# Two transformer blocks on one core: the norm's scale read from PSUM, weight splits issued earlier ahead of the norms, and a shared program end

## The reference, cut to what matters

```python
def rmsnorm(x, g):
    xf = x.astype(jnp.float32)
    y = xf * lax.rsqrt(jnp.mean(xf * xf, axis=-1, keepdims=True) + EPS)
    return (y * g.astype(jnp.float32)).astype(x.dtype)
...
    mix = jnp.einsum('bld,de->ble', merged, w_out)
    x = x + rmsnorm(mix, g_post_mix)
    h = rmsnorm(x, g_pre_mlp)
    ff = jnp.einsum('blf,fd->bld', jnp.square(jax.nn.relu(jnp.einsum('bld,df->blf', h, w_ff1))), w_ff2)
    return x + rmsnorm(ff, g_post_mlp)
```

## Time and profile before

| what | us |
|---|---|
| median of three runs | 3706.79 |
| the profiled execution | 3706.02 |
| its span (first to last instruction) | 3704.3 |
| TensorE matmul busy | 3508.4 (95%) |
| VectorE busy | 1446.7 (39%) |
| ScalarE busy | 873.6 (24%) |
| GpSimd busy | 895.3 (24%) |

### The profile page before, as it was taken

How to read it: one execution, slowest core, us unless ns; L and a number is a source line. 1 busy time by engine, 2 the same in 40 slices (tenths; PEclk the granted TensorE clock), 3 DMA queues, 4 the chain that set the end, 5 groups by cost and what they waited for, 6 DMA issues and landing times. The chain is left out here.

```text
span 3704.3 us, 40483 instructions
## 1 busy us (share of the span) xinstructions
PE 3508.4 (95%) x16092; PEld 2820.4 (76%) x16092; DVE 1446.7 (39%) x1591; ACT 873.6 (24%) x1068; POOL 895.3 (24%) x421
## 2 busy tenths in 40 slices
PE   6989999998998999999989998999999899999996
PEld 5767788887876888888867877777777588888885
DVE  7723565655315222212153446463552521121123
ACT  3112222223313111111232222212342411111111
POOL 2101111111341222222312114231245222222223
PEclk9979999999999999999999999999999999999998
DMA  2534343324421111111224213113253211111122
GB/s 109 148 70 158 109 147 126 100 88 167 146 91 73 47 45 51 45 51 45 91 97 124 92 66 120 63 69 125 99 199 136 74 45 51 45 51 45 45 79 102
DMA packets 105056, 336.81 MB, mean 91 GB/s; under 512 B 15232, under 2 KB 25344, under 8 KB 104848
## 3 DMA queue, kind: packets, MB, share of 16 engines
q1 hardware_dynamic: 101344, 329.78, 26.4%
q10 hardware_dynamic: 3584, 5.25, 0.5%
HBM read 250.37 MB, written 87.62 MB: 91 GB/s over the span
## 5 line engine op out<-in xcount | busy, mean ns | idle before, releaser
L270 POOL TENSOR_TENSOR w_lo<-w_raw,w_hi 128x1024 fp32r<-128x1024 f32 x276 | 686.6, 2488 | 2492.2 <-ACT w_hi L268 2492.2
L307 PE MATMUL pair<-act_hi,w_hi 128*128 128x512 f32 x2992 | 971.4, 406 | 18.9 <-issue 7.0
L307 PE MATMUL pair<-act_lo,w_hi 128*128 128x512 f32 x2992 | 946.5, 397 | 0.0
L307 PE MATMUL pair<-act_hi,w_lo 128*128 128x512 f32 x2992 | 945.1, 397 | 0.0
L307 PEld LDWEIGHTS pair<-act_lo,w_hi 128*128 128x128 f32 x2992 | 566.4, 189 | 138.6
L307 PEld LDWEIGHTS pair<-act_hi,w_lo 128*128 128x128 f32 x2992 | 565.4, 189 | 138.7
L307 PEld LDWEIGHTS pair<-act_hi,w_hi 128*128 128x128 f32 x2992 | 547.7, 190 | 142.7 <-issue 23.5
L268 ACT CAST w_hi<-w_raw 128x1024 fp32r<-128x1024 f32 x276 | 288.9, 1047 | 785.9 <-PE pair L307 709.6
L571 DVE TENSOR_TENSOR p<-pair,rs 128x1024 f32<-128x1024 f32 x100 | 122.1, 1221 | 435.6 <-PE pair L307 428.5
L1791 DVE TENSOR_TENSOR f2v<-pair,rs 128x1024 f32<-128x1024 f32 x42 | 51.4, 1224 | 346.6 <-PE pair L307 346.6
L307 PE MATMUL pair<-f1hh,w_hi 128*128 128x512 f32 x480 | 147.8, 389 | 0.0
(11 more groups left out here) (464 smaller groups left out, 4086.6 us busy)
## 6 DMA issues: line engine op xcount, KB each, us to landing
w_raw<-in_stream SPq DMA_DIRECT2D x278, 512.0 KB, 3.5
proj<-p SPq DMA_DIRECT2D x101, 512.0 KB, 2.6
m2g<-proj SPq DMA_DIRECT2D x32, 512.0 KB, 4.7
foxx<-proj SPq DMA_DIRECT2D x32, 256.0 KB, 5.5
m1g<-proj SPq DMA_DIRECT2D x16, 512.0 KB, 3.3
x<-f1y SPq DMA_DIRECT2D x16, 512.0 KB, 2.6
act_lo<-x SPq DMA_DIRECT2D x16, 512.0 KB, 7.8
m1l<-mixed SPq DMA_DIRECT2D x12, 512.0 KB, 9.2
```

What stands on the lines that cost most here:

```text
L270: nc.gpsimd.tensor_tensor(wlo[:, slot, :], raw[:, slot, :], whi[:, slot, :].bitcast(F32), ALU.subtract).then_inc(s_split, 1)
L307: last = nc.tensor.matmul(out_pair[:, h * HALF:(h + 1) * HALF], wt, a[:, h * HALF:(h + 1) * HALF], start=k == 0 and n_pass == 0, stop=k == ...
```

## The change

It has six parts.

1. In `bridge`, ScalarE's copy of the spread scale to SBUF goes; VectorE's multiplication reads the PSUM bank.
2. `stage` and `products` get `ahead`. With it, the split of unit b+2 is issued at the end of unit b's products, ahead of its eviction, in place of at the start of unit b+1. It is on for the stages of six blocks (three turns of two) in front of each bridge. The tail's second split then is already issued (`split=True`).
3. The splits in `TwoBlocks` are four subtractions of 256 columns each on GpSimd.
4. In `mix_out`, the tail's half-blocks are copied out of PSUM by ScalarE in place of VectorE.
5. `lag` of half 1 is 8 in place of 4: all eight tiles of the head's second block come after the last step.
6. Bridge 4 (no `next_gain`) multiplies by gain and scale in one instruction and then adds the residual, blocks 1, 3 and 5 of each half on GpSimd; stores go out by half-rows; the last square goes straight to TensorE and is not added by GpSimd; and `final=True` drops the splits and fetches of units that nothing uses.

```diff
+    def split_unit(b, slot, fills, pieces=1):
...
+        n = KT * P // pieces
+        for at in range(0, KT * P, n):
+            last = nc.gpsimd.tensor_tensor(wlo[:, slot, at:at + n], raw[:, slot, at:at + n],
+                                           whi[:, slot, at:at + n].bitcast(F32), ALU.subtract)
+        last.then_inc(s_split, 1)
...  in products
+                    if not ahead:
+                        split_unit(b + 1, 1 - slot, i * (per_turn // 2) + ((base + n // 8 + 1) // 2 + 1))
...
+                if ahead and (w == 7 or (not packed and k == tiles - 1)):
+                    split_unit(b + 2, slot, i * (per_turn // 2) + ((base + n // 8 + 2) // 2 + 1))
                 yield
             evict(i, o, out_pair, ready, reads.mark)
...  in stage
+        if ahead:
+            b = used["units"] + 1
+            split_unit(b, b % 2, b // 2 + 1)
...  in TwoBlocks.tile
-                split_unit(b + 1, 1 - slot, (b + 1) // 2 + 1)
-                fetch_unit(b + 3, 1 - slot)
+                if not self.split:
+                    split_unit(b + 1, 1 - slot, (b + 1) // 2 + 1, 4 if b else 1)
+                if not self.final:
+                    fetch_unit(b + 3, 1 - slot)
...
-                    if o == 0:
-                        split_unit(b + 2, slot, b // 2 + 2)
+                    if o == 0 and not self.final:
+                        split_unit(b + 2, slot, b // 2 + 2, 4)
...  in bridge
-        y_scale = [A.mark(A.after(spread).copy(r[:, halves[0]], bank[0][:])), None]
+        y_scale = [spread, None]
...
-        lag = (2, 4)
+        lag = (2, KT)
...  in add
-            V.mark(V.after(y_scale[h]).tensor_tensor(yk, yk, r[:, half], ALU.mult))
+            if not next_gain:
+                scaled = V.mark(V.after(y_scale[h], x_ready[k]).scalar_tensor_tensor(yk, yk, col(gain, k), bank[h][:],
+                                                                                     ALU.mult, ALU.mult))
+                if k in (1, 3, 5):
+                    added[h, k] = G.mark(G.after(scaled, x_ready[k]).tensor_tensor(yk, yk, x(k)[:, half], ALU.add))
+                else:
+                    added[h, k] = V.mark(V.then().tensor_tensor(yk, yk, x(k)[:, half], ALU.add))
+                SP.wait_ge(*added[h, k])
+                stores[k % 2].mark(SP.dma_start(out_dram[k][:, half], yk))
+                return
+            V.mark(V.after(y_scale[h]).tensor_tensor(yk, yk, bank[h][:], ALU.mult))
...
+            if k == 2 and not next_gain:
+                half_sums(bank[1][:], squares[:, halves[1]], True, False, summed)
+                sums = half_sums(bank[1][:], last_square[0], False, True, last_square[1])
...
-                y_scale[1] = A.mark(A.after(spread).copy(r[:, halves[1]], bank[1][:]))
+                y_scale[1] = half_spread(1, bank[1][:], root)
...  in mix_out
-            square_sum(dst, sq[:, half], squares[:, half], read(V.after(ready).tensor_copy(dst, psum)))
+            square_sum(dst, sq[:, half], squares[:, half], read(A.after(ready).copy(dst, psum)))
...
+        stage(3, 2, 2, KT, rhs, evict, per={A: 2, G: 2}, ahead=True)
...  in mlp
+                if not next_gain and o and half.start:
+                    a = read(V.after(ready).tensor_tensor(dst, dst, psum, ALU.add))
+                    last_square.extend([sq[:, half], A.mark(A.after(a, G.last()).activation(sq[:, half], dst, ACT.Square))])
+                    return
```

More of the change, by code:

```diff
@@ L269, in split_unit @@
         nc.gpsimd.wait_ge(s_whi, b + 3)
-        nc.gpsimd.tensor_tensor(wlo[:, slot, :], raw[:, slot, :], whi[:, slot, :].bitcast(F32),
-                                ALU.subtract).then_inc(s_split, 1)
+        n = KT * P // pieces
[3 more added lines that the diff above has]
+        last.then_inc(s_split, 1)
     def fetch_unit(b, slot):
@@ L282, in first_split, with products @@
         fetch_unit(2, 0)
-    def products(i, base, per_turn, n_out, tiles, rhs, evict):
+    def products(i, base, per_turn, n_out, tiles, rhs, evict, ahead=False):
         packed = n_out * tiles == 8 * per_turn
@@ L313, in products, with stage @@
                     ready = PE.mark(last)
+                if ahead and (w == 7 or (not packed and k == tiles - 1)):
+                    split_unit(b + 2, slot, i * (per_turn // 2) + ((base + n // 8 + 2) // 2 + 1))
                 yield
             evict(i, o, out_pair, ready, reads.mark)
-    def stage(turns, per_turn, n_out, tiles, rhs, evict, per=None):
+    def stage(turns, per_turn, n_out, tiles, rhs, evict, per=None, ahead=False):
+        if ahead:
+            b = used["units"] + 1
+            split_unit(b, b % 2, b // 2 + 1)
         if turns == 1:
@@ L326, in stage @@
             with loop(nc, turns, per) as i:
-                for _ in products(i, used["units"], per_turn, n_out, tiles, rhs, evict):
+                for _ in products(i, used["units"], per_turn, n_out, tiles, rhs, evict, ahead):
                     pass
@@ L391, in _build, with __init__ @@
     class TwoBlocks:
-        def __init__(self, tiles, rhs):
-            self.tiles, self.rhs = tiles, rhs
+        def __init__(self, tiles, rhs, split=False, final=False):
+            self.tiles, self.rhs, self.split, self.final = tiles, rhs, split, final
             self.base, self.begun = used["units"], False
@@ L463, in half_spread, with bridge @@
         return PE.mark(last)
-    def bridge(tail, tail_evict, y, squares, x, x_ready, r, sq, gain, out_dram, next_gain, head=None, head_evict=None):
+    def bridge(tail, tail_evict, y, squares, x, x_ready, sq, gain, out_dram, next_gain, head=None, head_evict=None,
+               last_square=None):
         halves = [slice(h * HALF, (h + 1) * HALF) for h in range(2)]
@@ L532, in bridge @@
             if k == 6:
-                spread = half_spread(1, bank[1][:], root)
-            if k == 7:
-                y_scale[1] = A.mark(A.after(spread).copy(r[:, halves[1]], bank[1][:]))
+                y_scale[1] = half_spread(1, bank[1][:], root)
         if next_gain:
@@ L1714, in __init__ @@
             self.x = sb(at, name + "v", [P, 2, L])
-        def scale_row(self):
-            return self.x[:, 1, :]
         def square_row(self, h, n):
@@ L1740, in tail_evict @@
             dst = y[:, 6 + o, half]
-            square_sum(dst, sq[:, half], squares[:, half], read(V.after(ready).tensor_copy(dst, psum)))
-        stage(3, 2, 2, KT, rhs, evict, per={A: 2, G: 2})
-        bridge(TwoBlocks(KT, act_rhs), tail_evict, y, squares, lambda k: late.hl[:, k, :].bitcast(F32), x_ready,
-               late.scale_row(), late.square_row, gain, out_dram, next_gain, TwoBlocks(KT, act_rhs), head_evict)
+            square_sum(dst, sq[:, half], squares[:, half], read(A.after(ready).copy(dst, psum)))
+        stage(3, 2, 2, KT, rhs, evict, per={A: 2, G: 2}, ahead=True)
+        bridge(TwoBlocks(KT, act_rhs, split=True), tail_evict, y, squares, lambda k: late.hl[:, k, :].bitcast(F32), x_ready,
+               late.square_row, gain, out_dram, next_gain, TwoBlocks(KT, act_rhs), head_evict)
     def first_hidden(late, gated):
@@ L1829, in hidden_rhs @@
                 return hh[:, k, :], hl[:, k, :]
-            stage(3 if final else 4, 2, 2, tiles, hidden_rhs, evict, per={A: 2, G: 2} if final else None)
+            stage(3 if final else 4, 2, 2, tiles, hidden_rhs, evict, per={A: 2, G: 2} if final else None,
+                  ahead=final)
             if not final:
@@ L1834, in mlp @@
                     e.wait_ge(s_mm, used["units"] + 2)
-        tail = TwoBlocks(tiles, hidden_rhs)
+        last_square = []
+        tail = TwoBlocks(tiles, hidden_rhs, split=True, final=not next_gain)
         bridge(tail, tail_evict, acc, squares, lambda k: act_lo[:, k, :].bitcast(F32), x_ready,
-               late.scale_row(), late.square_row, gain, out_dram, next_gain,
-               TwoBlocks(KT, act_rhs) if next_gain else None, head_evict)
+               late.square_row, gain, out_dram, next_gain,
+               TwoBlocks(KT, act_rhs) if next_gain else None, head_evict, last_square)
     def first_rows(dst, row, buf):
@@ L1991, in _stream @@
         parts += [w1[g:g + m], np.pad(w2[:, g:g + m], ((0, 0), (0, 8 - m), (0, 0), (0, 0)))]
-    tiles = np.concatenate([p.reshape(-1, P, P) for p in parts] + [np.zeros((3 * 8, P, P), np.float32)])
+    tiles = np.concatenate([p.reshape(-1, P, P) for p in parts] + [np.zeros((8, P, P), np.float32)])
     return _units(tiles)
```

6 lines of the change are left out of this document (2 added, 4 removed).

## The result

The changed kernel takes 3684.71 us (median of five runs, 3683.0 to 3687.99), the kernel before 3706.55 in five runs beside it: a ratio of 0.9944 (95% interval 0.9929 to 0.9958), 21.8 us less. Forecast were 3682.0 us and a range of 3672 to 3696. The span of the profiled execution, the fastest of its five (3683.0 us), went from 3704.3 to 3681.5 us, 22.8 less, against 25.0 forecast.

The account below looks back on a forecast made before the run. It took TensorE, 95% busy, as the bound, so only waits of TensorE or VectorE in the bridges counted. Bridge gains of 4.5, 6.9, 3.8 and 9.8 sum to 25.0 us: median 3682 us, range 3672 to 3696.

Parts of the forecast that it names:

- The tails: At the four tails: waits for `w_lo` go, TensorE's tail shifts by 1.9, 3.7, 1.9 and 5.1 us, 12.6 in all.
- the 1.7 us booked for the clock of bridge 2: Bridge 2, behind the tail's wait for `w_lo`: work lost to a clock of 0.78 for 7.7 us comes back, 1.7 us.
- the PSUM rival: Bridges: multiplications reading PSUM but writing SBUF still wait for GpSimd; 13 us given back, 3695 us; chance 0.08.
- the high end of 1.5 us: Bridge 4: a fused multiplication with a PSUM operand, taken at 0.75 us, might take up to 1.5, costing 12 us.
- the remaining wait is some 2 us, and I book half, 0.8: Half 0, bridge 1: the wait for `act_lo` 1 shrinks from 3.7 us; half of 1.7 us lost clock returns, 0.8.
- 4.8 forecast: Bridge 1, half 0: `act_lo` of block 1 arrives at 1125.1 in place of 1129.9, a gain of 4.8 us.
- the bound to the end of half 0: Bridge 1, after `act_lo` 1 and 0.3 us lost in the next block: TensorE bounds half 0; 4.5 us reach half 1.
- one of the rivals: Half 0, bridges 1 to 3: GpSimd goes ahead of every SBUF operation; 7.5 us lost, 3689 us; chance 0.16.
- The lag: End of bridges 1 to 3: `act_lo` 6 to the spread takes 8.7 us in place of 7.3, losing 1.4 each.
- The 0.7 us booked for bridge 3's clock: End of bridge 3: more idle time in steps 4 to 7 may lower the clock, a loss of 0.7 us booked once.
- Bridge 4: Last bridge: tail shift 5.1, copies 1.2, half 0 2.7, half 1 0.4, last store 0.4; gain 9.8 us.
- The rival called slower by the clock: Half 1, bridges 1 to 3: clock falls to 1.2 GHz from step 4 to the spread; 39 us lost, 3716; chance 0.04.

Follow-up runs that it names:

- tails_only: The kernel before with only the early splits ahead of the four tails added: 3697.99 us (nine runs), ratio 0.9972.
- late_splits: The changed kernel with the splits ahead of the tails issued late again, as in the kernel before: 3696.48 us, ratio 0.9964.
- fill: The changed kernel plus eight throwaway matmuls behind step 0 of half 0 in bridges 1 to 3, in TensorE's wait for `act_lo` 1: 3680.32 us, ratio 0.9931.
- one_piece: The changed kernel with every head split as one GpSimd subtraction of 1024 columns in place of four of 256: 3685.76 us, ratio 0.9944.
- lag4_fill_both: The changed kernel with lag 4, fill's matmuls and more throwaway matmuls in half 1 of bridges 1 and 3: 3674.11 us (four runs), ratio 0.9906.

## Why the prediction was right, and where it was wrong

**The tails** (part 2): right in mechanism, and 13.6 us measured against 12.6. The waits are gone, and the clock of 1.00 behind the tail in bridges 2 and 4 came as said. Both readings of 13.6, the change's and tails_only's, are against one trace of the kernel before. Against late_splits the sum is 13.5, but bridge 2 has 2.3 of it where 3.7 were forecast and bridge 3 has 3.7 where 1.9 were: the 1.7 us booked for the clock of bridge 2 belong to one execution, and that the two sums agree is partly luck.

**The copies and PSUM** (part 1): right. 0.69 us for a multiplication beside GpSimd's work and 0.75 for the fused one, so neither the PSUM rival nor the high end of 1.5 us came. In half 1 of bridge 2 the change has -0.71 = -1.38 (lag) + 0.67 (copy and the rest).

**Half 0 of bridges 1 and 3**: here the step failed that reads "the remaining wait is some 2 us, and I book half, 0.8". The wait was as forecast; its consequence had the wrong sign. Instead of a clock loss halved, the clock was at 0.50 through two more steps. Half 0 of bridge 1 took 28.07 us against 25.70 with the wait filled, so the fall cost 2.37 us there and 2.31 in bridge 3, where 0.8 of the earlier loss was to come back and about 0.9 to stay.

From the bridge's start to the second spread the account for bridge 1 closes. It gained 2.61 us where 5.3 was forecast: 4.92 by the arrival of `act_lo` 1 (4.8 forecast), less 0.93 of a wait for `act_lo` 2 (0.3), less 1.4 that I put down to the clock, where 0.8 stood with the opposite sign. I had scaled the loss with the length of the wait. The runs show no such scaling. The 3.7 us wait had cost about 1.3 us, an estimate: from `act_lo` 1 to the second spread the kernel before took 15.62 us without a wait, and fill 15.52 with one of 1.21. In tails_only, behind the same wait of 3.65 us, half 0 of bridges 1 and 2 took 0.8 and 1.0 us more still, and that of bridge 3 no more. The changed kernel took 17.93 us with a wait of 0.93, so its fall cost about 2.7, and 1.3 less 2.7 is the 1.4. Against the half's length with the wait filled, the 2.06 us wait cost from nothing to 2.4.

A second step failed by less. Fill's 2.82 and 2.86 us of gain in half 0 are 0.6 short of 3.4 though the whole clock loss is gone there. With the clock kept TensorE waits another 1.21 us for `act_lo` 2, of which 0.3 was booked: it is not "the bound to the end of half 0". The sentence on one of the rivals, that ScalarE's queue hides about 2 us, fits the result that one_piece costs nothing there. That rival says that the earlier trace rows show VectorE and GpSimd taking turns; those rows have no GpSimd row. The trace bears it out: GpSimd's split ended at 1120.08 and VectorE's multiplication at 1120.63, then GpSimd's sum at 1121.77 and VectorE's addition at 1122.32.

**The lag**: 1.4 us as forecast; from `act_lo` 6 to the spread bridge 2 takes 8.8 us (8.7 forecast), bridges 1 and 3 take 10.2 and 10.5 at the lower clock. The 0.7 us booked for bridge 3's clock were 1.55 by lag4_fill_both, so this term was less than half of what the fall costs.

**Bridge 4**: 10.7 against 9.8; every term within 0.4 us. Only the additions on GpSimd and the early splits were undone by themselves. The fused multiplication, the last square and the smaller stores are read from rows and not shown one by one.

**The sum**: 19.35 us in the bridges against 25.0. The span's 22.8 came close only because the untouched stretches were 3.45 us shorter, in code that the change leaves as it was: luck, not forecast. By the median, 21.8 us, the forecast is 3 us off. The rival called slower by the clock named the right mechanism in the wrong half, and at 13 us a bridge where it costs 2.4.

Left open: why the same stream of instructions with the same wait shows the fall in one execution and not in another, and what sets the clock outside the bridges.

## What to carry to other kernels

A wait in front of a stretch in which TensorE is the bound is to be priced with the clock behind it, and the length of the wait does not say how much: where the clock fell behind a 2 us wait, the half gained 2.3 to 2.4 us once that wait was filled with matmuls that nobody needs, or split by queue order into two of 1.6 and 1.7 us. Judge a change inside one stretch by that stretch's length in the trace; a median carries the scatter of all the others. And undo each part of a bundle by itself: of six parts, two (the lag, and the eviction on ScalarE) cost time under the cover of the rest. One trace does not show what the clock does: the same instructions with the same waits kept it in one execution and lost it in another.
